# Who makes the weights' remainders in an expert stage on one core: GpSimd or VectorE

## The reference, cut to what matters

```python
def block(hb):
    q = (hb @ wq).reshape(PEER_BLOCK, PEER_HEADS, 2, PEER_DKEY // 2)
    s = jnp.einsum('thsd,snd->thsn', q, subkeys)
    ...
    idx = e1 * PEER_KEYS + e2
    gate = jax.nn.softmax(sc, axis=-1)
    u_sel = u_tab[idx]
    v_sel = v_tab[idx]
    act = jax.nn.gelu(jnp.einsum('td,thkd->thk', hb, u_sel), approximate=False) * gate
    return jnp.einsum('thk,thkd->td', act, v_sel)
```

## Time and profile before

| | |
|---|---|
| median of 3 runs | 4432.41 us (4425.69 to 4434.58) |
| profiled execution | 4433.32 us, of it 4431.5 us span |
| TensorE / VectorE / ScalarE / GpSimd busy | 91% / 62% / 32% / 51% of the span |
| mean granted clock of TensorE | 0.955 |
| expert stage | from about 1290 to 2520 us |
| L244 in the whole program | x502, 1306.6 us busy, mean 2617 ns |
| L236 (ScalarE rounds a weight tile) | x502, mean 1047 ns |
| L1945, L1935 (gathered rows on VectorE) | x127, mean 3050 ns; x128, mean 2346 ns |

### The profile page before, as it was taken

The page is one execution under the profiler, slowest core; times in us unless marked ns, Lnnn a source line. Parts: engine busy times, 40 slices in busy tenths (PEclk is TensorE's granted clock), DMA queues, the critical chain, the costliest instruction groups (busy, mean ns, idle before and its releaser), DMA issues.

```text
span 4431.5 us, 50065 instructions
## 1 busy us (share of the span) xinstructions
PE 4011.8 (91%) x19979; PEld 3208.5 (72%) x19979; DVE 2752.2 (62%) x4203; ACT 1419.0 (32%) x2405; POOL 2255.8 (51%) x1268
## 2 busy tenths in 40 slices
PE   7988989998777888888989799998999989889998
PEld 4777755468666777887878675777888868656886
DVE  5686755448958999989988825526343440455334
ACT  4212211023863222222222325534222232443222
POOL 3155423134978888888888631023222345435443
PEclk9998999999888999999999899999999989999999
DMA  7100300242348888878887601011222212002231
GB/s 262 57 29 16 116 29 29 96 147 77 138 171 275 281 281 283 286 276 286 298 292 265 213 30 31 1 44 58 62 62 62 62 43 67 20 15 81 91 95 53
DMA packets 191332, 562.86 MB, mean 127 GB/s; under 512 B 16283, under 2 KB 66651, under 8 KB 188540
## 3 DMA queue, kind: packets, MB, share of 16 engines
q1 hardware_dynamic: 151100, 405.83, 27.2%
q0 software_dynamic: 40000, 153.84, 9.8%
HBM read 530.24 MB, written 29.36 MB: 126 GB/s over the span
## 4 chain that ended last, share of the span: by engine, by line
PE 44%; DVE 22%; issue 6%; POOL 6%; ACT 4%; DMA 2%; DVEq 0%; SPq 0%; POOLq 0%; ACTq 0%
PE psum L260 11%; PE psum L254 11%; PE psum L256 11%; PE psum L255 11%; DVE tok L1945 6%; DVE selrow L1935 5%; DVE junk L1957 3%; POOL pair L244 2%; POOL o L1841 1%; ACT Ah L2009 1%; DVE psum L1924 1%; PE psum L355 1%; DVE Al L1926 1%; DVE raw_ring L1959 1%; DMA selrow<-peerrow,hiU 1%
## 5 line engine op out<-in xcount | busy, mean ns | idle before, releaser
L244 POOL TENSOR_TENSOR pair<-raw_ring,pair 128x1024 fp32r<-128x1024 f32 x502 | 1306.6, 2617 | 1320.2 <-ACT pair L236 1267.4
L236 ACT CAST pair<-raw_ring 128x1024 fp32r<-128x1024 f32 x502 | 512.1, 1047 | 379.7 <-PE psum L256 316.1
L254 PE MATMUL psum<-pfh,pair 128*128 128x384 f32 (+1 forms) x1152 | 416.7, 362 | 121.8 <-DVE Al L1926 101.0
L255 PE MATMUL psum<-pfl,pair 128*128 128x384 f32 (+1 forms) x1152 | 409.2, 355 | 0.0
L256 PE MATMUL psum<-pfh,pair 128*128 128x384 f32 (+1 forms) x1152 | 409.0, 355 | 0.0
L254 PE MATMUL psum<-ffh,pair 128*128 128x512 f32 (+1 forms) x1056 | 379.5, 359 | 16.7 <-DVE ffl L2150 15.7
L1945 DVE SCALAR_TENSOR_TENSOR tok<-selrow,best,tok 128x1024 f32<-128x1024 f32 x127 | 387.4, 3050 | 7.1 <-DMA selrow<-peerv,hiU 0.2
L255 PE MATMUL psum<-ffl,pair 128*128 128x512 f32 (+1 forms) x1056 | 379.1, 359 | 0.0
L256 PE MATMUL psum<-ffh,pair 128*128 128x512 f32 (+1 forms) x1056 | 379.1, 359 | 0.0
L254 PEld LDWEIGHTS psum<-pfh,pair 128*128 128x128 f32 x1152 | 228.8, 199 | 147.2 <-issue 113.5
L254 PE MATMUL psum<-pair,Ah 128*128 128x512 f32 x768 | 307.8, 401 | 22.7 <-POOL pair L244 19.2
(11 more groups left out here) (643 smaller groups left out, 9130.4 us busy)
## 6 DMA issues: line engine op xcount, KB each, us to landing
raw_ring<-wmod SPq DMA_DIRECT2D x144, 512.0 KB, 5.5
raw_ring<-peeru SPq DMA_DIRECT2D x128, 512.0 KB, 3.8
raw_ring<-peerv SPq DMA_DIRECT2D x128, 512.0 KB, 4.6
raw_ring<-win SPq DMA_DIRECT2D x48, 512.0 KB, 4.2
gates<-stage SPq DMA_DIRECT2D x12, 2048.0 KB, 7.2
Gb<-gates SPq DMA_DIRECT2D x32, 768.0 KB, 9.3
raw_ring<-wgate SPq DMA_DIRECT2D x44, 512.0 KB, 3.5
raw_ring<-wup SPq DMA_DIRECT2D x44, 512.0 KB, 3.5
```

The lines of the kernel that those rows point to most:

```text
L236: ac.e.copy(self.pair(t)[0], k.R.of(t)).then_inc(*k.A.up("hi", t))
L244: po.e.tensor_tensor(lo, k.R.of(t), hi.bitcast(F), ALU.subtract).then_inc(*k.G.up("lo", t))
L254: e.matmul(out, w[0], x[0], start=first, stop=False, skip_group_check=True)
L255: e.matmul(out, w[0], x[1], start=False, stop=False, skip_group_check=True)
```

## The change

VectorE makes the remainders of the tiles V 0 to 127 and U 17 to 127 (`AHEAD` = 17): 128 + 111 = 239 of the 502. GpSimd skips them. All others stay with GpSimd. Arithmetic, rounding, tile order, pairs, ring and DMAs are the same. `split`, by which TensorE waits, now names VectorE's count for these tiles, and the ring's place is freed by it.

```diff
@@ class Weights
+    def by_vector(self, t):
+        return t[0] == "V" or t[0] == "U" and t[1] >= AHEAD
+
     def split(self, name):
-        return self.k.G.at("lo", name)
+        return (self.k.V if self.by_vector(name) else self.k.G).at("lo", name)
...
         for t in self.when[name]:
+            if self.by_vector(t):
+                continue
             hi, lo = self.pair(t)
...
+    def vector_lo(self, dv, name):
+        k = self.k
+        for t in self.when[name]:
+            if not self.by_vector(t):
+                continue
+            hi, lo = self.pair(t)
+            dv.wait_ge(k.A.at("hi", t))
+            dv.e.tensor_tensor(lo, k.R.of(t), hi.bitcast(F), ALU.subtract).then_inc(*k.V.up("lo", t))
+            k.R.over(t, k.V.now())
@@ def vector_experts
+    for n in range(FIRST + len(BESIDE), AHEAD):
+        k.W.vector_lo(dv, ("U", n))
     up(0)
     up(1)
     for gi in range(NG):
         rows = chosen_rows(gi)
         for i, t in enumerate((2 * gi, 2 * gi + 1)):
+            if AHEAD <= t + 2 < 128:
+                k.W.vector_lo(dv, ("U", t + 2))
             if 0 <= t - MODS < 98:
                 mods(t - MODS)
             if t + 2 < 128:
                 up(t + 2)
             for s in rows[2 * i:2 * i + 2] if i == 0 else rows[2:]:
                 row(s)
+        for n in (2 * gi, 2 * gi + 1):
+            k.W.vector_lo(dv, ("V", n))
```

## The result

The changed kernel takes 4272.8 us (median of 4 runs, 4269.9 to 4277.8) against 4429.1 us for the kernel before on the same chip (4424.6 to 4434.6): ratio 0.965, 95% interval 0.963 to 0.967, or 156 us less. The forecast was 4298 us in a range of 4262 to 4352. The profiled execution took 4277.8 us, its span 4276.0 us, 155.5 us less than the span before. Here is where they went.

| stretch | before, us | after, us | difference | forecast |
|---|---|---|---|---|
| up to the first gates of group 1 | 1331.7 | 1337.1 | +5.5 | 0 |
| groups 1 to 7 | 103.9 | 88.2 | -15.7 | -17 |
| groups 8 to 40 | 661.7 | 566.4 | -95.3 | -74 |
| groups 41 to 56 | 307.2 | 261.3 | -45.9 | -35 |
| groups 57 to 61 | 89.0 | 83.6 | -5.4 | -5 |

A forecast was written before the change was run, and what follows sets the result against it. It took the alternation of VectorE and GpSimd on SBUF reads to bound groups 8 to 40. Savings of 17, 48, 26, 40 and 4 us by stretch made -135 us: 4433 to 4298 us, range 4262 to 4352.

The forecast's parts named there:

- The bound: Groups 8 to 40: VectorE and GpSimd alternate on two-input SBUF reads, 18.7 us of a 19.79 us group.
- The new instruction: VectorE's 239 added remainders, 1024 columns wide: 1.14 to 1.22 us each, with 1.52 us as upper bound.
- Rival 2: The new instruction is dear, 1.52 us each: 48 us less gain, 4346 us; chance 0.1, shared with thinner overlap.
- The sum: Whole kernel: the stretches' savings add up to -135 us, so 4433 us become 4298 us.
- Groups 8 to 40: VectorE still bounds, at 17.8 then 18.3 us a group including added waits: -48 and -26 us.
- Groups 41 to 56: TensorE bounds at 16.95 us a group, 0.2 of it added: -38 us, and +3 for TensorE's smaller lead.
- Groups 1 to 7: VectorE needs 10.1 us a group, taken as 12 for waits on gathered rows: 101 us become 84, -17.
- Before group 1: V 0 and V 1 move ahead of the first gates, which wait for ScalarE's last GELUs anyway: 0 us.
- The end: `X`'s reload can be issued some 17 us before TensorE's end; TensorE's last product and copies are late next: -4 us.
- The waits: VectorE's new waits for ScalarE's rounding are free, with some 1 us to spare at group heads from 41 on.
- Rival 1: Transfers become the bound, no group under 18.8 us (304 GB/s): -77 us, 4356 us; chance 0.2.
- Rival 4: GpSimd can't issue indirect DMAs beside VectorE: 34 us a group, about +780 us, 5200 us; chance 0.05 including milder forms.

The follow-up runs named there:

- the second experiment: Changed kernel, with GpSimd also filling a spare buffer with zeros, reading nothing, at some 220 of the moved remainders' places: 4273.2 us, ratio 0.964.
- 54 copies: Changed kernel plus 54 device-memory copies of 512 KB, two with each load of `Gb`, on SyncE's queue: 4276.3 us, ratio 0.965.
- the first experiment: Changed kernel, with GpSimd also doing some 220 subtractions on constant tiles at the moved remainders' places, results unused: 4649.6 us, ratio 1.049.
- the run with V moved: Changed kernel with only the V tiles' remainders on VectorE, those of U 17 to 127 back on GpSimd: 4323.4 us, ratio 0.977.
- 108 copies in fours: Changed kernel plus 108 device-memory copies of 512 KB, four with each load of `Gb`, on SyncE's queue: 4392.6 us, ratio 0.990.
- one by one: Changed kernel plus 108 device-memory copies of 512 KB, one after each tile's rounding, on ScalarE's queue: 4310.4 us, ratio 0.972.

## Why the prediction was right

**The bound.** Right from group 8 on, where most of the gain is. TensorE was late because VectorE was, and VectorE because it and GpSimd took turns; putting GpSimd's reads back costs 377 us, putting its work back without the reads next to nothing. In groups 1 to 7 it was not `Al` that came late but the remainders (20.4 against 1.8 us of TensorE's waiting), which the prediction, with one row of waits, didn't see. The account of one group (18.7 of 19.79 us taking turns) had a hole that changed nothing: it left out that VectorE also has 3.1 us of gates, of which some 2 us ran beside GpSimd's turns.

**The new instruction.** Right: forecast 1.14 to 1.22 us from the half-wide row and the pitch, measured 1.22 us and a pitch of 1.14. Rival 2 (1.52 us, 4346 us) is out, by 239 cases at 1.22 us; L837's median in the earlier trace rows is of a stretch in which GpSimd computes beside it.

**The sum.** From group 8 on the mechanism was right, and the sum was 20 us short of the 155.5 measured. Term by term:
- *Groups 8 to 40*, forecast -74, measured -95.3. (The split of the forecast at group 31 is off by one group: 471 us were 23 groups and 191 us ten, so -48 and -26 are not what they are called; the sum of the two isn't touched.) The mis-sized term is "I add about 0.5 us a group for such waits where VectorE bounds". There were none: the floors of 17.25, 12.5 and 17.9 us came out as means of 17.25 (17.10, and 18.25 in the groups with five rows), 11.45 and 17.6. The addition was 23 x 0.55 + 1.5 + 9 x 0.4 = 18 of the 21 us missed. Every wait had been costed at nothing in the text, with its cover; then a lump was added all the same.
- *Groups 41 to 56*, forecast -35, measured -45.9. The term that failed is 16.95 us for every group from 41 on: in groups 41 to 44 VectorE's 15.16 to 15.22 us a group still set the pace, while TensorE used up the lead it had, and only from 45 on did it take 16.72. 4 x 1.78 = 7 us are the first four groups, 12 x 0.23 = 3 us the others, in which the added 0.2 us wasn't there either. That covers the 11 us (the +3 for a smaller lead and the stretch's true 307.2 us, for 309, make up the rest).
- *Groups 1 to 7*, -17 and -15.7, right in size, in part by luck. The forecast was 101 us becoming 84; measured were 103.9 and 88.2, both higher. Six of the seven groups take 11.5 us in the mean, near the 12 taken, and the seventh 19.3, with five remainders, five rows and the first two dot products in it. The waits for rows, the reason given for 12 us and not 10.1, are 7.4 us in all seven groups, 1.1 a group.
- *Before group 1*, forecast 0, measured +5.5. 3.4 us are real: three V remainders, which stand at the end of group 0 (from 1333.71 to 1337.12), lie between its last row and the first gates of group 1, and nothing covers them. The other 2.1 us is that the gates of group 0 begin later in this execution (1325.91 against 1323.85); with the same order they began at 1321.33 in the second experiment's trace, so this is scatter.
- *The end*, -4 and -3.3, right in size, wrong in its reason. Forecast: the reload of `X` is issued some 17 us ahead of TensorE's end. It was issued 7.7 us ahead of it (2349.32 and 2357.0), for GpSimd keeps the remainders of the next two weight tiles, and the reload stands behind them. Two rows of the chain of waits of after (start, us, what):

```profile
2345.99 3.33 POOL pair L250
2349.32 9.34 DMA X<-hkeep
```

and VectorE's timeline there:

```profile
2358.69 5.36 DVE L2012 SCALAR_TENSOR_TENSOR X<-psum,mods,X 128x512 f32<-128x512 f32 x8 [0.79 <-DMA X<-hkeep]
```

  So the reload is still the last to arrive, by 0.79 us, where it had been by 4.27; "X's reload no longer in the chain" was wrong, and the next thing late, TensorE's copies, lies right behind it, so that it cost nothing; that is luck.
- *The rest*: +4.5 us in a part of the program that is the same. In the thirteen traces it lasted between 1908.8 and 1918.9 us, so this is scatter, as large as the uncertainty of any one term here.

**The waits.** The reasons held as written. At the head of a group, while VectorE bounds, U's rounding is long done (the three L261 of 1643.02 run in one piece). V behind two rows is free (1635.61 follows without a gap). VectorE nowhere waits for `raw_ring` in the stage, and for `selrow` only 7.4 us, in groups 1 to 7. When TensorE bounds, "free, with some 1 us to spare" came out too: VectorE's timeline at two even tiles' gates, one group apart, in the fourth stretch:

```profile
2085.96 0.57 DVE L1941 TENSOR_TENSOR psum<-psum,Gb 128x384 f32<-128x384 f32 x1 [1.16 <-ACT psum L2026]
...
2102.68 0.57 DVE L1941 TENSOR_TENSOR psum<-psum,Gb 128x384 f32<-128x384 f32 x1
```

16.72 us, TensorE's own, with a pause of 1.16 us on VectorE.

**Rival 1, transfers.** Closer than its chance of 0.2 says, and not because of the mean: DMA is 88 to 95% busy in groups 8 to 56. The scaled figure of 341 GB/s was no ceiling (with 54 copies it is 362), nor was 398 GB/s for 10 us one that lasts: that is about 376 GB/s for this mix. The margin against TensorE is 1.5 us a group, if the loads are even (16.72 less 15.2).

**Rival 4, GpSimd can't issue.** Out, as the earlier trace rows said: in the group shown two issues take 1.68 and 1.98 us beside VectorE's unbroken instructions, and VectorE's stay at 1.22.

**Not foreseen: the clock.** The floors were reckoned at full clock, from the earlier trace rows, and TensorE had 0.96 in groups 8 to 40 before. That the dense stretch would get 1.00 was assumed without a word, and came true. By an estimate (16.72 / 0.96) TensorE's group would be 17.4 us at 0.96, and it would have bound in place of VectorE in groups 8 to 30.

## What to carry to other kernels

Where two engines take turns at a resource, price a piece of work by how long it holds the resource on each of them, here 1.14 us on VectorE against 2.35 us on GpSimd, and not by which engine has time to spare; GpSimd was the one with spare time before this change, and using it was what cost. If every wait has been costed at nothing with its cover named, believe it or name the wait that fails, but don't add a lump; and when the bound passes from one engine to another, count the groups in which the old lead is used up. Once the work is moved, look for work on the new bound that can be done in another stretch: moving 17 dot products to where VectorE had time gave 13 to 15 us more.

## What the runs showed of the hardware that was not expected

**Turns are not always given one by one.** In the kernel before, at the start of the full groups, VectorE's instruction was held through nearly four subtractions in a row. VectorE's and GpSimd's timelines of before:

```profile
1418.03 10.15 DVE L1935 CUSTOM_DVE_ANT_0 selrow<-selrow,htok 128x1024 f32<-128x1024 f32 x1 [1.50 <-DMA selrow<-peerrow,hiU]
```
```profile
1417.77 9.32 POOL L244 TENSOR_TENSOR pair<-raw_ring,pair 128x1024 fp32r<-128x1024 f32 x4
```

VectorE asks at 1418.03 and is through at 1428.18, 1.09 us after GpSimd's fourth ends at 1427.09. That is no strict alternation, as the prediction had it: where GpSimd has its next instruction ready it may go first. In other places (and the rows of the first experiment) GpSimd's instructions take 2.9 to 3.1 us each and one of VectorE's gets in between. In the run with V moved a dot product starts at 1585.13, 0.32 us ahead of GpSimd's pair, and still ends 1.09 us behind its second. What decides wasn't tried.

**GpSimd's issue of an indirect DMA waits for VectorE, but doesn't hold it.** It takes 0.93 us at best and 1.68 to 1.98 us in most cases beside two-input instructions of VectorE, which stay at 1.22 us.

**A burst costs more than its bytes.** 108 copies in fours made 4392.6 us, one by one 4310.4 us, at 348 and 376 GB/s. (They were also issued by another engine, so the spacing alone isn't shown to be the cause.)
